# An expert pass in another order, its first weight chunk in two 1 MB transfers

## The reference, cut to what matters

```python
def expert_block(args):
    xb, e = args
    gu = xb @ w_gate_up[e] + b_gate_up[e]
    gate = jnp.minimum(gu[:, :D_FF], SWIGLU_LIMIT)
    up = jnp.clip(gu[:, D_FF:], -SWIGLU_LIMIT, SWIGLU_LIMIT)
    act = (up + 1) * gate * jax.nn.sigmoid(gate * SWIGLU_ALPHA)
    return act @ w_down[e] + b_down[e]
...
contrib = y_rows[dest] * sorted_gate[:, None]
out = jnp.zeros_like(xt).at[sorted_tok].add(contrib)
...
y_prompt = rms_norm(xp, norm_final_g)
y_sample = rms_norm(xs, norm_final_g)
```

## Time and profile before

| | us |
|---|---|
| median of 3 runs | 1279.43 |
| runs | 1278.24 to 1279.56 |
| profiled execution, its own time | 1279.69 |
| its span | 1277.9 |
| PE busy in the span | 1247.8 |
| before the first expert pass | 290.2 |
| the 36 passes | 290.2 to 1263.9 |
| what follows the last pass | 1263.9 to 1277.9 |

### The profile page before, as it was taken

The page is one execution under the profiler, slowest core; times in us unless marked ns, Lnnn a source line. Parts: engine busy times, 40 slices in busy tenths (PEclk is TensorE's granted clock), DMA queues, the critical chain, the costliest instruction groups (busy, mean ns, idle before and its releaser), DMA issues.

```text
span 1277.9 us, 17340 instructions
## 1 busy us (share of the span) xinstructions
PE 1247.8 (98%) x6433; PEld 546.2 (43%) x6434; DVE 501.1 (39%) x1007; ACT 206.2 (16%) x403; POOL 37.5 (3%) x63
## 2 busy tenths in 40 slices
PE   9999999999999999999999999999999998999996
PEld 7656754663333433334333333333343333333332
DVE  3743545466433323333233333333243333243344
ACT  1032223561101110011010011100010100011102
POOL 2000002400000000000000000000000000000000
PEclk9999999999999999999999999999999999999998
DMA  9531234338999979999979999996999999699994
GB/s 331 214 132 67 83 135 133 141 132 321 428 427 427 405 289 428 428 427 428 427 330 378 428 428 427 427 428 280 423 427 428 427 426 426 263 428 427 426 427 200
DMA packets 48026, 436.33 MB, mean 341 GB/s; under 512 B 6245, under 2 KB 7389, under 8 KB 19334
## 3 DMA queue, kind: packets, MB, share of 16 engines
q1 hardware_dynamic: 44000, 429.41, 80.8%
q0 software_dynamic: 2080, 6.48, 1.5%
q10 hardware_dynamic: 1926, 0.18, 0.1%
HBM read 432.33 MB, written 3.72 MB: 341 GB/s over the span
## 4 chain that ended last, share of the span: by engine, by line
PE 83%; DMA 13%; DVE 2%; issue 1%; ACT 0%; SPq 0%; POOL 0%; DVEq 0%; POOLq 0%
PE PS L1916 34%; PE PS L1956 16%; DMA ring<-in_w_gate_up_dram 13%; PE PS L1377 6%; PE PS L1386 5%; PE PS L1874 4%; PE PS L1331 4%; PE PS L1842 4%; PE PS L1388 1%; PE PS L1420 1%; PE PS L1710 1%; PE PS L1899 1%; PE PS L1684 1%; PE PS L1568 1%; PE PS L1336 1%
## 5 line engine op out<-in xcount | busy, mean ns | idle before, releaser
L1916 PE MATMUL PS<-ring,r 128*64 128x512 f32 x2304 | 520.3, 596 | 12.3 <-DMA ring<-in_w_gate_up_dram 11.8
L1916 PEld LDWEIGHTS PS<-ring,r 128*64 128x64 f32 x2304 | 158.6, 137 | 315.6 <-issue 280.8
L1956 PE MATMUL PS<-ring,r 128*64 128x512 f32 x1152 | 255.1, 595 | 0.3
L1200 DVE SCALAR_TENSOR_TENSOR r<-PS,gprev,r 128x512 f32<-128x512 f32 (+1 forms) x222 | 152.5, 741 | 114.4 <-PE PS L1874 112.6
L1956 PEld LDWEIGHTS PS<-ring,r 128*64 128x64 f32 x1152 | 82.1, 137 | 148.4 <-issue 146.0
L1303 DVE TENSOR_TENSOR yy<-PS,yy 128x512 fp32r<-128x512 f32 x36 | 24.9, 692 | 249.8 <-ACT yy L760 249.8
L1286 DVE TENSOR_SCALAR r<-PS 128x512 f32<-128x512 f32 x36 | 24.9, 692 | 202.7 <-PE PS L1916 202.7
L749 ACT ACTIVATE r<-r 128x512 f32<-128x512 f32 x36 | 22.7, 629 | 505.5 <-DVE r L1286 505.5
L1331 PE MATMUL PS<-ident,r 128*128 128x128 f32 (+4 forms) x491 | 81.1, 293 | 0.9 <-ACT e L528 0.4
L1874 PE MATMUL PS<-yy,place 64*128 64x512 f32 x444 | 71.8, 428 | 2.6 <-ACT yy L760 1.6
L1331 PEld LDWEIGHTS PS<-ident,r 128*128 128x128 f32 (+4 forms) x491 | 61.2, 182 | 26.8 <-DVE r L1293 15.2
(11 more groups left out here) (331 smaller groups left out, 786.3 us busy)
## 6 DMA issues: line engine op xcount, KB each, us to landing
ring<-in_w_gate_up_dram SPq DMA_DIRECT2D x96, 2048.0 KB, 16.3
ring<-in_w_down_dram SPq DMA_DIRECT2D x64, 2048.0 KB, 16.8
ring<-in_w_gate_up_dram SPq DMA_DIRECT2D x64, 1024.0 KB, 16.2
ring<-in_w_in_dram SPq DMA_DIRECT2D x7, 2048.0 KB, 15.5
ring<-in_w_out_dram SPq DMA_DIRECT2D x3, 2048.0 KB, 7.5
ring<-in_w_in_dram SPq DMA_DIRECT2D x2, 1024.0 KB, 9.0
r<-in_x_prompt_dram SPq DMA_DIRECT2D x2, 512.0 KB, 3.9
r<-in_x_prompt_dram POOLq DMA_DIRECT2D x2, 512.0 KB, 4.5
```

What stands on the lines that cost most here:

```text
L1200: v.scalar_tensor_tensor(xx, PS[0:rows, out_banks(t)[h], :], gprev[0:rows, t:t + 1], xx, ALU.mult, ALU.add)\
L1916: last = mm(PS[64 * h:64 * h + 64, m, :], xt[:, k % 4, k // 4, :], w[:, kk, D * m + 512 * h:D * m + 512 * h + 512], start=False, stop=(k = ...
L1956: last = mm(PS[64 * h:64 * h + 64, 2, :], at[:, kk, c, :], w[:, kk, 512 * h:512 * h + 512], start=(c == 0 and kk == 0), stop=(c == 1 and k ...
```

## The change

In the pass: c0 comes as two transfers of 1 MB, each with its own arrival (`w_full[1]`, `latter_full`) and its own release (`gs_half` after the first half, `gs_used` after the second). The bias products go behind c0. The gather goes ahead of c3. The whole combine goes behind c3; row tile 2, which has 64 rows, now holds its two column halves on the two halves of the partitions, so that its combine is 2 products with 128 rows of weights instead of 4 with 64, and its accumulate one operation of 512 columns instead of two. The combine writes banks that the clamps read: it waits for `g_ready` ahead of tile 1 and for `up_ready` ahead of tile 2. `turn` goes ahead of `places`. Clamp of the gate, sigmoid and product run in halves of 256 columns. The sums of DVE come in the order 3, 0, then the scaling of the gathered rows, then 1, 2, 4.

Around it: one PSUM memset more ahead of the first one-hots, the first placement copied in three ACT and four DVE operations instead of one and two, one copy of gates and one copy of rows more, two more transfers of the final gain, a last combine by parts (high parts as soon as they are there), a final norm of tile 2 on 512 columns with three more small ACT operations, two output transfers for it instead of one. Some semaphores of the front are merged.

```diff
@@ SP
+                if c == 0:
+                    slot = ring[:, EXPERT_SLOT[c], :].rearrange("p (k n) -> p k n", k=k)
+                    sp.dma_start(slot[:, 0:1, :], rows[:, h, k0:k0 + 1, :]).then_inc(w_full[EXPERT_SLOT[c]], 16)
+                    if first is not None:
+                        sp.wait_ge(s["gs_used"], first)
+                    sp.dma_start(slot[:, 1:2, :], rows[:, h, k0 + 1:k0 + 2, :]).then_inc(latter_full, 16)
-            used = ["gs_used", "gs_used1", "gs_used2", "gu_mm", "ds_used", "d_mm"]
+            used = ["gs_half", "gs_used1", "gs_used2", "gu_mm", "ds_used", "d_mm"]
...
-            sp.dma_start(y_sample[0, :, :], xn[0:SS, 2, :]).then_inc(s["y_out"], 16)
+            for h in range(2):
+                sp.dma_start(y_sample[0, :, 512 * h:512 * h + 512], xn[64 * h:64 * h + 64, 2, 0:HALF]).then_inc(s["y_out"], 16)
@@ ACT
-            a.activation(place[:, 0:TC], PS[:, 4, 0:TC], ACT.Copy).then_inc(s["c_ready"], 1)
+            a.activation(place[:, 0:256], PS[:, 4, 0:256], ACT.Copy)
+            for h in range(2):
+                last = a.activation(place[64 * h:64 * h + 64, 256 + 64 * h:320 + 64 * h], PS[64 * h:64 * h + 64, 4, 256:TC], ACT.Copy)
+            last.then_inc(s["c_ready"], 1)
+            a.activation(x[64:128, 2, 0:HALF], x[0:SS, 2, HALF:D], ACT.Copy).then_inc(s["rows_split"], 1)
             def expert_pass(b):
-                act.wait_ge(s["g_ready"], b + 1)
-                a.activation(sg, ug, ACT.Sigmoid, scale=ALPHA).then_inc(s["sig_ready"], 1)
-                act.wait_ge(s["ct_mm"], b + 1)
-                act.wait_ge(s["comb_mm"], 6 * b + 6)
-                a.activation(place[:, :], PS[:, 5, 0:128 * NT], ACT.Copy).then_inc(s["c_ready"], 1)
                 act.wait_ge(s["xe_mm"], b + 2)
                 a.activation(xe, bank(3), ACT.Copy).then_inc(s["xe_ev"], 1)
+                for q in range(2):
+                    part = slice(256 * q, 256 * q + 256)
+                    act.wait_ge(s["g_ready"], 2 * b + q + 1)
+                    a.activation(sg[:, part], ug[:, part], ACT.Sigmoid, scale=ALPHA).then_inc(s["sig_ready"], 1)
+                act.wait_ge(s["ct_mm"], b + 1)
+                act.wait_ge(s["comb_mm"], 5 * b + 5)
+                a.activation(place[:, :], PS[:, 5, 0:128 * NT], ACT.Copy).then_inc(s["c_ready"], 1)
@@ DVE
+            step(v.memset(PS[:, 5, 256:384], 0.0))
             positions_of(0, 0)
             first_one_hots(0)
...
             for low in (NE, 3 * NE):
-                v.tensor_tensor(place[low:low + NE, 0:TC], PS[low:low + NE, 4, 0:TC],
-                                place[low:low + NE, 0:TC].bitcast(f32), ALU.subtract).then_inc(s["gates_held"], 1)
+                step(v.tensor_tensor(place[low:low + NE, 0:256], PS[low:low + NE, 4, 0:256],
+                                     place[low:low + NE, 0:256].bitcast(f32), ALU.subtract))
+                own_cols = slice(256, TC) if low == NE else slice(TC, 384)
+                v.tensor_tensor(place[low:low + NE, own_cols], PS[low:low + NE, 4, 256:TC],
+                                place[low:low + NE, own_cols].bitcast(f32), ALU.subtract).then_inc(s["gates_held"], 1)
...
                 dve.wait_ge(s["gates_held"], b + 2)
-                accumulate(6 * b, 0)
-                accumulate(6 * b, 1)
                 dve.wait_ge(s["ct_mm"], b + 1)
...
-                dve.wait_ge(s["gs_used"], b + 1)
+                dve.wait_ge(s["gs_used1"], b + 1)
                 selector(e_next)
                 dve.wait_ge(s["gate_mm"], b + 1)
-                v.tensor_scalar(ug, bank(0), LIMIT, None, ALU.min).then_inc(s["g_ready"], 1)
-                dve.wait_ge(s["sig_ready"], b + 1)
-                v.tensor_tensor(sg, sg, ug, ALU.mult).then_inc(s["glu_ready"], 1)
+                for q in range(2):
+                    part = slice(256 * q, 256 * q + 256)
+                    v.tensor_scalar(ug[:, part], bank(0)[:, part], LIMIT, None, ALU.min).then_inc(s["g_ready"], 1)
+                for q in range(2):
+                    part = slice(256 * q, 256 * q + 256)
+                    dve.wait_ge(s["sig_ready"], 2 * b + q + 1)
+                    dve.wait_ge(s["g_ready"], 2 * b + 2)
+                    v.tensor_tensor(sg[:, part], sg[:, part], ug[:, part], ALU.mult).then_inc(s["glu_ready"], 1)
...
-                accumulate(6 * b, 2)
-                dve.wait_ge(s["o_ev"], 6 * b + 8)
+                accumulate(5 * b, 3, OUT_BANKS)
+                accumulate(5 * b, 0, OUT_BANKS)
+                gathered(b + 1)
+                for i in (1, 2, 4):
+                    accumulate(5 * b, i, OUT_BANKS)
+                dve.wait_ge(s["o_ev"], 5 * b + 7)
                 v.tensor_copy(gprev[:, :], pg[:, bass.ds(e, 1), NT:2 * NT].rearrange("p a n -> p (a n)"))\
                     .then_inc(s["gates_held"], 1)
-                gathered(b + 1)
@@ PE
+            def spread(t, part, banks):
+                if t == 2:
+                    last = mm(bank(banks[4]), place[:, 256:384], yy2[:, part, :], start=(part == 0), stop=(part == 1))
+                    if part:
+                        last.then_inc(s["comb_mm"], 1)
+                    return
+                for h in range(2):
+                    half = slice(64 * h, 64 * h + 64)
+                    last = mm(bank(banks[2 * t + h]), place[half, 128 * t:128 * t + 128], yy2[half, part, :],
+                              start=(part == 0), stop=(part == 1))
+                    if part:
+                        last.then_inc(s["comb_mm"], 1)
+            def combine(b):
+                if isinstance(b, int):
+                    pe.wait_ge(s["route_ready"], 1)
+                pe.wait_ge(s["yyl_ready"], b + 2)
+                pe.wait_ge(s["c_ready"], b + 2)
+                pe.wait_ge(s["o_ev"], 5 * (b + 1) + 2)
+                for t in range(NT):
+                    if t == 1:
+                        pe.wait_ge(s["g_ready"], 2 * (b + 1) + 2)
+                    if t == 2:
+                        pe.wait_ge(s["up_ready"], b + 2)
+                    for part in range(2):
+                        spread(t, part, OUT_BANKS)
+            def combine_last(b):
+                pe.wait_ge(s["c_ready"], b + 2)
+                pe.wait_ge(s["o_ev"], 5 * (b + 1) + 2)
+                for part in range(2):
+                    pe.wait_ge(s[("yy_ready", "yyl_ready")[part]], b + 2)
+                    for t in range(NT):
+                        spread(t, part, LAST_BANKS)
...
                 pe.wait_ge(s["xt_ev"], b + 1)
-                pe.wait_ge(s["sel_ready"], b + 1)
-                for m in range(2):
-                    for h in range(2):
-                        mm(PS[64 * h:64 * h + 64, m, :], sel[:, :], b_gu3[:, D * m + 512 * h:D * m + 512 * h + 512],
-                           start=True, stop=False)
+                if not beside:
+                    pe.wait_ge(s["o_ev"], 5 * b + 2)
                 for c in range(GU_CHUNKS):
+                    if c == 1:
+                        pe.wait_ge(s["sel_ready"], b + 1)
+                        for m in range(2):
+                            for h in range(2):
+                                mm(PS[64 * h:64 * h + 64, m, :], sel[:, :],
+                                   b_gu3[:, D * m + 512 * h:D * m + 512 * h + 512], start=False, stop=False)
...
-                    if c == outputs:
-                        combine(b - 1, 0)
-                        combine(b - 1, 1)
+                    if c == GU_CHUNKS - 1:
+                        if beside:
+                            gather_first(1)
+                        else:
+                            gather(b + 1)
...
                         for kk in range(2):
+                            if c == 0 and kk == 1:
+                                last.then_inc(s["gs_half"], 1)
+                                pe.wait_ge(latter_full, 16 * n + 16)
...
-                        combine(b - 1, 2)
                         for kk in range(2):
                             last = gate_up(kk, 1)
                         last.then_inc(s["gu_mm"], 1)
-                if beside:
-                    gather_first(1)
-                else:
-                    gather(b + 1)
+                combine(b - 1)
                 pe.wait_ge(s["act_ready"], b + 1)
                 pe.wait_ge(s["at_ev"], b + 1)
...
+                turn(b + 1)
                 pe.wait_ge(s["c_ready"], b + 2)
                 places(b + 1)
-                turn(b + 1)
                 pe.wait_ge(s["at_ev"], b + 2)
+                pe.wait_ge(s["o_ev"], 5 * b + 3)
```

More of the change, by code:

```diff
@@ L1137, in _ @@
             add_att(3)
-            step(v.memset(place[:, TC:128 * NT].bitcast(f32), 0.0))
+            step(v.memset(place[:, 256:128 * NT].bitcast(f32), 0.0))
             step(v.memset(zeros32, 0.0))
@@ L1975, in _ @@
             with pe.Fori(1, total) as b:
[L1976 to L1978 removed]
+                expert_pass(b, pe.value_load(turn_of[0:1, bass.ds(b, 1)], min_val=0, max_val=NE - 1))
```

(1 more changed line is left out.)

130 lines of the change are left out of this document (66 added, 64 removed).

## The result

| | before | after |
|---|---|---|
| median, 7 runs each | 1279.56 us | 1283.76 us |
| ratio, 95% interval | | 1.0026 (1.0017 to 1.0035) |
| profiled execution, own time | 1279.69 us | 1283.80 us |
| its span | 1277.9 us | 1282.0 us |

The change makes the kernel 0.26% slower by the ratio; the two medians lie 4.2 us apart.

A forecast was written before the change was run, and what follows sets the result against it. PE and the transfers were both near their limit, each bounding some stretches. PE-bound passes -0.7, first pass +1.35, three transfer-bound stretches +1.2 and tail -1.1 gave +0.75 us: 1280.2 us in the median, range 1275.5 to 1284.

The forecast's parts named there:

- the part to which I gave 0.27: Whole kernel: the outcome slower than within 0.2% (1276.9 to 1282.0 us), given chance 0.27.
- rival B: Each pass: the gate's halves come too late for the clamp of up; 4.3 us slower, 1284.4 us; chance 0.22.
- the forecast's own range: Whole kernel: 1278 to 1283 us around the forecast of 1280.2 us, without the rivals; chance 0.59.
- my signs of being wrong: Profile: a pass under 26.3 or over 26.6 us, no holes and shorter stretches, or chunk waits in the last 6 passes.
- The first pass: First pass: PE waits 1.2 us for the one-hots, plus a 0.2 us memset; +1.35 us (+0.1 to +1.9).
- The tail: Behind the last pass: one sum less, shorter scaling, earlier combine, one more output request; -1.1 us (-0.4 to -1.6).
- The period: Where passes wait for chunks: 29.44 us per expert before, 29.5 us forecast with the second split chunk.
- The way behind c2: End of a transfer-bound stretch: c2 becomes the last waited chunk, with more PE work behind it; +0.4 us a stretch.
- Rival A: Transfer-bound stretches: the transfers use the whole early start; 1273.9 us, or 1275.4 with the split as measured; chance 0.17.
- rival C: All transfers: each extra one pays 2.2 us although the queue is full; 46 us slower, 1326 us; chance 0.02.
- step 2: Transfer-bound stretch, from S (start of a double's second pass): early release lets c4 start sooner; -0.5 us (0 to -2.1).
- the eleven passes: PE-bound passes 1 to 5 and last 6: each 26.45 us instead of 26.51; -0.7 us together (-2.2 to +1.1).

The follow-up runs named there:

- E2: The changed kernel with c0 as one whole transfer again, bias products still behind it: 1280.53 us, 0.9994 of the kernel before.
- E8: The changed kernel with c0 whole and the bias products in front of it again: 1278.67 us, 0.9981 of the kernel before.
- E10: E2 once more, measured beside E11: 1280.10 us, 0.9997 of the kernel before.
- E3: The changed kernel with c0 still in two transfers, both requested only when the whole chunk is used: 1282.35 us, 1.0009 of the kernel before.
- E1: The changed kernel measured again without edit: 1286.33 us, 1.0042 of the kernel before.
- E7: The changed kernel with c0 whole, the loop's gather ahead of c2 and the first pass's gather behind c3: 1275.60 us, 0.9954 of the kernel before.
- E11: E8 once more, measured beside E10: 1278.97 us, 0.9987 of the kernel before.
- E12: E7 with the bias products in front of c0: 1275.35 us, 0.9957 of the kernel before.
- E6: The kernel before with only c0's split and early release added, some front semaphores merged: 1283.68 us, 1.0012 of the kernel before.
- E9: The changed kernel, c0 still split with early release, with the bias products in front of c0: 1284.06 us, 1.0037 of the kernel before.

## Why the prediction was right or wrong

The time, 1283.76 us, lies in the range (1275.5 to 1284), in the part to which I gave 0.27; my likeliest time, 1280.2, was 3.6 us too low, and 'no difference that can be measured' was too likely. That it lies in the range is luck: the forecast's own range ended at 1283, the rest was there for rival B, and B did not come. Two of my signs of being wrong came as well, a pass under 26.3 us (26.18) and waits for chunks in the last six passes.

**What held.** Which stretches are set by what, in the kernel before. The first pass: +1.16 and +0.16 measured against +1.35. The tail: -1.14 against -1.1. The period: +0.08 us for each further split chunk; E2, E8 and E10 have 29.43 to 29.46 without it. Here the row of c3's halves decided rightly against the figure of the Trainium skill, "DMA: Bandwidth & Descriptors", "Bandwidth", of 6.15 us for 1 MB. In the stream 1 MB takes half of 4.98 us, and the first half of c0, requested with nothing in flight, landed 4.6 us after its request (2.07 to 6.7 behind the start of the pass), so the measurement decides here too. The way behind c2: +0.26 against +0.4. Rival A (the whole early start gained) and rival C (each transfer pays) did not come, and B is excluded by DVE's rows: two pipelined halves take 0.75 us where one operation on 512 columns takes 0.69. (The Trainium skill, "VectorE: DVE Perf Modes", "The TRN2 errata", which advises 512 elements or more, points the right way; here the price is 0.06 us and lies beside other work.)

**What failed first: step 2, "A stretch set by the transfers".** "c4 starts at S + 23.36 + L. Of 2.2 us of earlier start, 0.5 are left." I took L, the time from request to data, as the same whether the stream is full or about to run dry. It is not: c4 was requested about when I said (23.10 for 23.36) and landed on average 0.9 us later than the usual 31.5 instead of 0.5 us earlier. The start of the stream came forward, and the releases behind it did not; they then met a stream with little left in flight. Undoing only the early release (E3) took 4.0 us off E1, and in the 32 profiled restarts of kernels without it (before, E2, E3, E7, E8, E10, E11, E12) c4 landed 4.9 us behind c3, that is, without a pause. What in the chip makes up the pause was not measured. Nor is its size a function of the lead alone: c1 with 3.3 us of lead has a pause of 1.1 us in E2, with 2.6 us one of 0.4 us in the kernel before (one time 1.7 us), c4 with 3.0 to 3.3 us has none, and with 3.9 and 4.0 us it has 0.6 and 0.3 us in the changed kernel.

The table of restarts gives the sum for the three stretches. Behind c4's landing they took 0.69 us more each (forecast +0.9: the split and the way behind c2). c4's landing came 0.25 us later on average (forecast -0.5), and only because one of the three restarts of the kernel before was itself late (33.3); against its other landings it is 0.9 us. That is +2.82 for the forecast's +1.2.

**What failed second: "The first pass, passes 1 to 5, and the last 6 passes are bound by PE."** That is so before, and I carried it over. I saw the reserve ("about 0.6 us of lead") and put its loss into the range as "up to 1 us", while it was the likely case. PE's pass came out 0.33 us shorter, not 0.06, and the transfers later; the eleven passes had 3.6 us to gain and lost 1.1 us. The mechanism behind the pass was half right: the transposes of `ac` still wait for DVE. Of the 0.27 us that I missed, 0.19 is in the gate/up products (13.85 us for 14.04), where two changes of kind fell away that I had left out of the sum, about 0.1 us each; 0.13 is in the wait for `ac` (1.70 us for 1.83), since the clamp of up came 0.11 us sooner behind the up half; the transposes took 0.06 more.

**Which part costs what.** The split costs 1.8 us by medians (E3 against E2). The early release costs 4.0 us (E1 against E3, measured side by side; 2.2 us with the ratio of the first measurement), and nothing that shows in the old order (E6). The bias products behind c0 cost about 0.7 us in each stretch when c0 is whole, 1 to 2 us in all, and nothing that shows when c0 is split (E9). The rest of the rearrangement alone is a gain: E8 and E11 stand at 0.9981 and 0.9987. With the gather where PE waits anyway and c0 whole, E7 and E12 are 0.46% and 0.43% faster than the kernel before.

**Left open.** What sets the length of a pause; and whether c5, now the waited chunk, could be passed by using c4 and c5 in smaller pieces. Neither was tried. That the late landing of c4 comes from the small lead of its request is argued from the table; no run moved the request of c4 alone.

## What to carry to other kernels

When a ring of buffers is fed by a stream at its limit, do not ask how early the first transfer can start, but how far each later request lies ahead of the end of what is in flight; an early small piece in front can use up that reserve, as it did here in the new order and not in the old one. Cut the work behind the last waited transfer (put work that needs no new data into the wait), and re-check after each cut which transfer is now the last. And where an engine and the transfers are both near their limit, a gain on the one is to be counted only up to the reserve of the other.

## What was not expected of the hardware

Four bias products, 0.43 us of work, between the releases of c0 and c1 went with a pause of 0.9 to 1.6 us between their landings in eight of eight restarts (E2, E10); there was none in eight of eight without them (E8, E11). A chunk of 2 MB landed 7.2 us after its request with nothing in flight (c0 in E2 and E8), and 8.1 to 10.3 us after it in the six restarts of the changed kernel in which c4 was requested with 1.6 to 2.1 us of lead: longer, although less than half a chunk was ahead of it. The pauses ahead of c4 with the early release scattered from 0.3 to 3.2 us among eight restarts of one kernel.
